# A two-layer block and a tail layer on one core: the first two output slots of each mixer computed between attention units, in the projections' banks, and added to the residual fill by fill

## The reference

```python
for l in range(2):
    x = x + 0.5 * swiglu(rms_norm(x, ffn1_norm[l]), w_gate, w_up, w_down)     # d_ff = 2816
    h = rms_norm(x, mix_norm[l])
    pa, pb, pc, pd = split(h @ w_in[l])
    ya = neighbourhood_mixer(pa, ...)      # group A, 4 heads of 64
    yb = mla_mixer(pb, ...)                # group B
    yc = diff_mixer(pc, ...)               # group C
    yd = gqa_mixer(pd, ...)                # group D
    x = x + concatenate([ya, yb, yc, yd], axis=-1) @ w_out[l]                 # 1024 x 1024
    x = x + 0.5 * swiglu(rms_norm(x, ffn2_norm[l]), ...)
    x = rms_norm(x, final_norm[l])
```

## Time and profile before

| | us |
|---|---|
| median of 3 runs | 1333.03 |
| lowest and highest | 1330.23, 1341.21 |
| the profiled execution, its whole time | 1337.2 |
| the profiled execution, span from first to last instruction | 1334.9 |
| PE busy in the span | 1268.9 (95%) |
| DVE busy | 867.8 (65%) |
| ACT busy | 642.3 (48%) |
| mean granted clock of TensorE | 0.963 of 2.4 GHz |

### The profile page before, as it was taken

The page is one execution under the profiler, slowest core; times in us unless marked ns, Lnnn a source line. Parts: engine busy times, 40 slices in busy tenths (PEclk is TensorE's granted clock), DMA queues, the critical chain, the costliest instruction groups (busy, mean ns, idle before and its releaser), DMA issues.

```text
span 1334.9 us, 24675 instructions
## 1 busy us (share of the span) xinstructions
PE 1268.9 (95%) x10500; PEld 1243.0 (93%) x10500; DVE 867.8 (65%) x979; ACT 642.3 (48%) x850; POOL 80.4 (6%) x57
## 2 busy tenths in 40 slices
PE   6999999977999999999999996999999999899997
PEld 6999999967999999999999985899999999899896
DVE  5765677875666666876667786485666654547665
ACT  5433356844443334533336764453333554756542
POOL 1110011210000000000010320000000000000000
PEclk9999999975999999999999995899999999999999
DMA  8876665320466655566665530256665555325542
GB/s 283 231 213 209 199 201 178 102 89 1 158 200 198 197 192 189 168 203 200 195 213 148 175 115 13 69 185 199 197 197 194 189 166 187 98 65 159 171 147 108
DMA packets 169513, 220.33 MB, mean 165 GB/s; under 512 B 5280, under 2 KB 152480, under 8 KB 169312
## 3 DMA queue, kind: packets, MB, share of 16 engines
q1 hardware_dynamic: 165680, 213.66, 50.0%
q0 software_dynamic: 2080, 2.48, 1.0%
q10 hardware_dynamic: 1680, 3.13, 0.7%
HBM read 218.15 MB, written 3.42 MB: 166 GB/s over the span
## 4 chain that ended last, share of the span: by engine, by line
PE 81%; DVE 10%; ACT 5%; issue 2%; DMA 1%; SPq 0%; POOLq 0%; POOL 0%; DVEq 0%; ACTq 0%
PE pj L433 11%; PE pj L436 11%; PE pj L437 11%; PE acc L436 8%; PE acc L433 8%; PE acc L437 8%; PE tr L433 5%; PE tr L436 5%; PE tr L437 5%; PE acc L616 4%; ACT probs L994 2%; DVE w_lo L1186 2%; ACT w_hi L875 1%; PE tr L608 1%; PE acc L596 1%
## 5 line engine op out<-in xcount | busy, mean ns | idle before, releaser
L1186 DVE TENSOR_TENSOR w_lo<-raw,w_hi 128x2048 fp32r<-128x2048 f32 (+2 forms) x206 | 459.3, 2230 | 236.8 <-ACT w_hi L875 235.6
L875 ACT ACTIVATE w_hi<-raw 128x2048 fp32r<-128x2048 f32 (+2 forms) x206 | 381.1, 1854 | 395.1 <-PE pj L433 140.5
L433 PE MATMUL pj<-hT_hi,w_hi 128*128 128x256 f32 x992 | 277.2, 279 | 5.5 <-DVE scratch L1559 3.1
L436 PE MATMUL pj<-hT_lo,w_hi 128*128 128x256 f32 x992 | 275.6, 278 | 0.0
L437 PE MATMUL pj<-hT_hi,w_lo 128*128 128x256 f32 x992 | 275.6, 278 | 0.0
L437 PE MATMUL acc<-act_hi,w_lo 128*128 128x256 f32 x704 | 194.3, 276 | 0.0
L436 PE MATMUL acc<-act_lo,w_hi 128*128 128x256 f32 x704 | 194.3, 276 | 0.0
L433 PE MATMUL acc<-act_hi,w_hi 128*128 128x256 f32 x704 | 194.3, 276 | 0.0
L433 PEld LDWEIGHTS pj<-hT_hi,w_hi 128*128 128x128 f32 x992 | 187.3, 189 | 6.9 <-DVE scratch L1559 3.5
L436 PEld LDWEIGHTS pj<-hT_lo,w_hi 128*128 128x128 f32 x992 | 187.4, 189 | 0.0
L437 PEld LDWEIGHTS pj<-hT_hi,w_lo 128*128 128x128 f32 x992 | 187.1, 189 | 0.0
(11 more groups left out here) (213 smaller groups left out, 2016.3 us busy)
## 6 DMA issues: line engine op xcount, KB each, us to landing
raw<-in_w_in SPq DMA_DIRECT2D x47, 1024.0 KB, 5.3
raw<-in_ffn_w_up SPq DMA_DIRECT2D x44, 1024.0 KB, 5.3
raw<-in_ffn_w_down SPq DMA_DIRECT2D x44, 1024.0 KB, 5.0
raw<-in_ffn_w_gate SPq DMA_DIRECT2D x43, 1024.0 KB, 5.4
raw<-in_w_out SPq DMA_DIRECT2D x12, 1024.0 KB, 5.0
raw<-in_w_proj_a SPq DMA_DIRECT2D x4, 512.0 KB, 3.5
raw<-in_w_proj_b SPq DMA_DIRECT2D x4, 512.0 KB, 4.0
raw<-in_w_proj_c SPq DMA_DIRECT2D x4, 512.0 KB, 3.4
```

The costliest lines, as they stand in the source:

```text
L433: ins = pe.matmul(out, lhs[0], rhs[0], start=first, stop=False, **kw)
L436: pe.matmul(out, lhs[0], rhs[1], start=False, stop=False, **kw)
L875: act.activation(w_hi[r % RING][:, 0:w], raw[r % RING][:, 0:w], ACT.Copy).then_inc(hi_set, 1)
L1186: dve.tensor_tensor(w_lo[r % RING][:, 0:w], raw[r % RING][:, 0:w], w_hi[r % RING][:, 0:w].bitcast(F32), ALU.subtract).then_inc(lo_set, 1)
```

## The change

The steps of groups A and B move forward in `ORDER`: "prep yA" and "yturn A" stand around the scores of units 4 and 5, "wout A" between "soft 4" and "probs 4"; "prep yB" and "yturn B" behind "turn D", "wout B" between "soft 6" and "soft 7". They no longer add up in `acc`. A new function `out_pairs` computes each in four fills of the banks `pj`, two chunks of output channels in a fill (4 products, 12 matmuls), and DVE adds each fill to `xT` with one tensor_tensor of 128x512, behind its `look_ahead`. The transposed outputs of A and B are kept in `act_hi` and `act_lo` (as `br_hi`, `br_lo`) and no longer in `hT_hi`, `hT_lo`. In `acc` only C and D add up; `first` is now "C".

```diff
-         ("norm", "yA"), ("proj", 8), ("probs", 3), ("pv", 2), ("turn", "B"), ("pv", 3), ("norm", "D"),
-         ("score", 4), ("score", 5), ("prep", "D"), ("soft", 4), ("probs", 4), ("pv", 4), ("soft", 5),
-         ("probs", 5), ("pv", 5), ("score", 6), ("score", 7), ("turn", "D"), ("soft", 6), ("soft", 7),
-         ("probs", 6), ("prep", "yA"), ("norm", "yB"), ("probs", 7), ("pv", 6), ("pv", 7), ("norm", "yC"),
-         ("yturn", "A"), ("score", 8), ("score", 9), ("soft", 8), ("prep", "yB"), ("prep", "yC"),
-         ("soft", 9), ("probs", 8), ("probs", 9), ("pv", 8), ("pv", 9), ("yturn", "B"), ("norm", "yD"),
-         ("prep", "yD"), ("yturn", "C"), ("wout", "A"), ("wout", "B"), ("yturn", "D"), ("wout", "C"),
-         ("wout", "D")]
+         ("norm", "yA"), ("proj", 8), ("probs", 3), ("pv", 2), ("turn", "B"), ("pv", 3), ("norm", "D"), ("prep", "yA"),
+         ("score", 4), ("score", 5), ("yturn", "A"), ("prep", "D"), ("soft", 4), ("wout", "A"), ("probs", 4), ("pv", 4),
+         ("soft", 5), ("probs", 5), ("pv", 5), ("norm", "yB"), ("score", 6), ("score", 7), ("turn", "D"), ("prep", "yB"),
+         ("yturn", "B"), ("soft", 6), ("wout", "B"), ("soft", 7), ("probs", 6), ("probs", 7), ("pv", 6), ("pv", 7),
+         ("norm", "yC"), ("score", 8), ("score", 9), ("soft", 8), ("prep", "yC"), ("soft", 9), ("probs", 8), ("probs", 9),
+         ("pv", 8), ("pv", 9), ("yturn", "C"), ("norm", "yD"), ("prep", "yD"), ("wout", "C"), ("yturn", "D"), ("wout", "D")]
...
 def pj_fills(step):
+    if step in (("wout", "A"), ("wout", "B")):
+        return 4
...
+        def y_half(late, early, m, c):
+            return (early if m < 2 else late)[:, 2 * m + c, :]
...
+            def out_pairs(f0, wv, c0):
+                for d in range(DC):
+                    f = f0 + d // 2
+                    if d % 2 == 0:
+                        bank = begin_pj(f)
+                    for c in range(2):
+                        ins = product(bank[:, d % 2, :], wv(c, d * P, (d + 1) * P), (br_hi[:, c0 + c, :], br_lo[:, c0 + c, :]),
+                                      c == 0, c == 1, begins=(c + d == 0))
+                    if d % 2:
+                        ins.then_inc(pj_full[f % 2], 1)
...
-                        first, last = step == MIX_SLOTS[-4], step == MIX_SLOTS[-1]
+                        first, last = k == "C", k == "D"
...
-                        out_cols(wv, 2 * "ABCD".index(k), first, last)
+                        if k in "AB":
+                            out_pairs(pj_[step], wv, 2 * "AB".index(k))
+                        else:
+                            out_cols(wv, 2 * "ABCD".index(k), first, last)
...
-                        ins = act.activation(hT_hi[:, 2 * m + c, :],
+                        ins = act.activation(y_half(hT_hi, br_hi, m, c),
...
-                            hT_lo[:, j, :], tr[(f0 + m) % 2][:, 2 * c:2 * c + 2, :].rearrange("p a b -> p (a b)"),
-                            col(l, gain + j), hT_hi[:, j, :].bitcast(F32), ALU.mult, ALU.subtract)
+                            y_half(hT_lo, br_lo, m, c), tr[(f0 + m) % 2][:, 2 * c:2 * c + 2, :].rearrange("p a b -> p (a b)"),
+                            col(l, gain + j), y_half(hT_hi, br_hi, m, c).bitcast(F32), ALU.mult, ALU.subtract)
...
                     elif kind == "wout":
                         if step != ORDER[-1]:
                             look_ahead(SLOT_OF[step], l)
+                        if k in "AB":
+                            for q in range(4):
+                                f, two = pj_[step] + q, slice(2 * q, 2 * q + 2)
+                                wait_pj_full(dve, f)
+                                if k == "B":
+                                    wait_pj_free(dve, pj_[("wout", "A")] + q)
+                                dve.tensor_tensor(xT[:, two, :], pj[f % 2], xT[:, two, :], ALU.add).then_inc(pj_free[f % 2], 1)
...
+                for q in (2, 3):
+                    wait_pj_free(dve, pj_[("wout", "B")] + q)
                 take_over(3 * l + 2, FFN2_AT + 1, l, 1.0)
```

## The result

The changed kernel takes 1370.51 us (median of 4 runs, 1370.19 to 1374.79) against 1331.66 us before (4 runs): ratio 1.0283, 95% interval 1.0231 to 1.0336. It is slower by 38.9 us; forecast were 36.8. The profiled execution took 1370.2 us (span 1367.9), 33.0 more than that of before.

A forecast was written before the change was run, and what follows sets the result against it. In units 4 to 9 no engine is full, so queue order in the PE-DVE-ACT chain decides; elsewhere PE bounds. Layer terms +17.9 and +18.9, together +36.8 on the median 1333.03, gave 1370 us, range 1345 to 1387.

The forecast's parts named there:

- Unit 4 to the addition: Walk through layer 0's new order: wout A starts at 285.15, PE then waits 4.5 us or more for DVE's first addition.
- Unit 6's scores: Start of unit 6's scores, delayed by wout A's fills: +16.0 us in layer 0, +17.0 in layer 1.
- the way of transposes, copies and pv: Remaining way from wout A's fills to unit 6's scores: 9.9 us, between 7.4 at full clock and 12.3 at half.
- wout B: Units 6 and 7 with wout B between: unit 7's transposes later by +11.1 us, bounds +10.7 and +13.4.
- T+12.5: Start of wout B, 12.5 us after T, the start of unit 6's scores.
- From there to the last transposes: Between pv 7 and score 8, yturn A goes away with DVE's two low halves: -0.9 us.
- rival 1: Same chain, but the fills keep PE's clock full through the units: +6.8 us a layer, 1347 us; chance 12%.
- Tail: End of the mixer, only C and D left: 17.8 us against 26.1, so -8.3 us; bounds -5.3 and -10.
- the stall and its releaser: Sign: PE idle over 4 us between wout A's second and third fill, released by DVE's addition.
- the gaps absorb the fills: A's and B's fills lie in PE's idle time in the units, only the savings remain: 1315 us; chance 5%.

The follow-up runs named there:

- cut up by the gaps: Kernel before with only group A moved early, its fills, additions and look-ahead halves placed separately where engines idle; 1314.19 us, ratio 0.9882.
- the kept-busy runs: Kernel before plus 88, then 115, useless matmuls a layer in PE's idle times; 1320.72 us (ratio 0.9873) and 1314.54 us (0.9879).
- both mendings: Changed kernel with prep D moved behind wout A and the look-ahead put between the second and third addition; 1361.02 us, ratio 1.0187.

## Why the prediction was right

**Unit 4 to the addition.** The walk held to the tenth: wout A at 285.15 (measured 285.23), first addition at 294.1 (294.24), fill 2 at 294.85 (294.97), transposes of unit 4 at 299.4 (299.70). That the fall of the clock is where it was before showed too: wout A's first matmuls last 0.41 us and start 0.21 apart.

**Unit 6's scores**, said +16.0 and +17.0: measured +13.8 (307.15 for 293.34) and +15.5 (842.19 - 810.88 = 31.3 for 15.8). The term that was mis-sized is the way of transposes, copies and pv, put at 9.9, the middle of its bounds; it took 7.45, the bound at full clock: the last matmuls of the fills ahead of it were 0.12 us apart already.

**wout B**, said +11.1: unit 7's transposes stand 23.97 us after unit 6's scores in both layers, for 12.6, so +11.4. The walk's T+12.5 for wout B was T+12.4.

**From there to the last transposes**, said -0.9: measured -6.6 in layer 0 (345.68 - 331.12 = 14.6 for 21.15) and -3.4 in layer 1. Here part of rival 1 came in: with the clock at 0.89 in layer 0 after unit 7, pv 8 and pv 9 took 3.7 for 6.9. The rival had the mechanism, the forecast had not.

**Tail**, said -8.3: -8.1 in layer 0 (18.0 for 26.1) and -5.9 in layer 1. The sum for layer 0 came out by two errors that cancel: wout C ran at the full clock and took 5.7 us for the 7.1 said, and in wout D the clock fell (0.76), so that it took 7.15 for the 5.5 said. In layer 1 parts of both ran at the low clock.

Layer 0 makes 13.8 + 11.4 - 6.6 - 8.1 = +10.5, layer 1 15.5 + 11.4 - 3.4 - 5.9 = +17.6, for the 17.9 and 18.9 that I had. The other 4.9 of the profiled 33.0 lie outside the mixers; one place of them is the hand-over to layer 1, where the changed kernel's clock fell as it had not before (554 to 564 us: 0.60 and 0.72). So the mechanism was right, the stall and its releaser to the tenth, but that 1370 was met so closely is luck in good part. In the mixers the change cost 28.1 us and not 36.8, since the clock gave back more there than I allowed; 4.9 came from outside them, which I had not forecast; and of the last 5.9, from 33.0 to 38.9, nearly all comes from the profiled execution of before, which lay 5.5 us above its median.

**The rivals.** That the gaps absorb the fills (1315) was wrong for this order, for the reason given; cut up by the gaps, the very same fills of A bring 1314. For whether moved work costs or gains, its place decided and not the idle share. In the kernel before, the kept-busy runs took the clock of the window from 0.59 to 1.00. In the changed kernel the same means took it from 0.77 to 0.88 only and did not rescue it (ratio 1.0218 still), since its own waits were DVE's; a clock of 1.00 throughout was not reached there. The rule of the Trainium skill, TensorE: Matmul & The Clock Gate, Part 1, that sustained activity lifts the throttled clock, agrees with these windows.

Left open: what of the 1.9% that stay with both mendings belongs to each of its four named parts. No run takes one of them away alone. Open as well is how the 1.2% of the cut-up version divides between order and clock.

## What to carry to other kernels

Idle time of the engine that gets the new work says little; write out, for the engine that must free its buffer, what stands ahead of that freeing instruction in its queue. With two buffers and four fills, one unrelated 2.3 us instruction ahead of the first release cost 1.6% of the kernel (0.8 to 2.3%), and behind the second nothing that was measurable. Where work is moved into a chain's gaps, give producer, releaser and any preparation of later data separate places in the order.

## What the runs showed of the hardware

The granted clock in the sparse stretches was worth as much as the best reordering: 115 useless matmuls a layer, which took it from 0.59 to 1.00, made the kernel 1.2% faster (ratio 0.9879), and the version cut up by the gaps, at 0.81, came to 0.9882. And it makes sums of waits uncertain by some us: taking a wait of 5 us away shortened the way to unit 6's scores by 4.6 us and the whole stretch of layer 0 by nothing, as the clock around pv 8, pv 9 and wout C was 0.54 instead of 1.00.
